# Three transformer blocks on one Trainium2 core: unread products ahead of TensorE's waits, sigmoid gates in one pass, compressed scores in two steps

## The reference, cut to what matters

```
# block 1: x = x + gate_m * (mixed @ w_out);  then x = x + gate_f * MLP(...)
fox = rms(forgetting_attention(q, k, v)) * gain * sigmoid(f_og)
ret = rms(retention(rope(rq), rope(rk), rv)) * gain * silu(r_gate)
# block 2 (NSA): x = layer_norm(ALPHA*x + mix); x = layer_norm(ALPHA*x + MLP(x))
s_c = q . kc ; p_c = masked_softmax(s_c) ; o = g0*(p_c @ vc) + g1*selected + g2*window
# block 3 (GLA): o = rms(gla(q, k, v)) * norm_g ; mix = (o * silu(r)) @ w_out ; norms as in block 2
```

## Time and profile before

| | |
|---|---|
| median of 3 runs | 1013.54 us (1010.81, 1013.54, 1016.82) |
| the profiled execution | 1010.89 us, span 1009.1 us |
| TensorE busy | 964.6 us, 96% of the span |
| VectorE busy | 655.6 us, 65% |
| ScalarE busy | 485.2 us, 48% |
| mean granted TensorE clock | 0.985 of full |
| DMA | 185 GB/s mean |

### The profile page before, as it was taken

The page is one execution under the profiler, slowest core; times in us unless marked ns, Lnnn a source line. Parts: engine busy times, 40 slices in busy tenths (PEclk is TensorE's granted clock), DMA queues, the critical chain, the costliest instruction groups (busy, mean ns, idle before and its releaser), DMA issues.

```text
span 1009.1 us, 14960 instructions
## 1 busy us (share of the span) xinstructions
PE 964.6 (96%) x5618; PEld 826.8 (82%) x5618; DVE 655.6 (65%) x830; ACT 485.2 (48%) x734; POOL 53.9 (5%) x59
## 2 busy tenths in 40 slices
PE   9999979799999999999799999998999989999996
PEld 7778867699999987876599999996776879999995
DVE  5977897784555656566865555557644876554555
ACT  5566736454544444444345444534544635444540
POOL 3040101100000001000100000001000010000000
PEclk9999989999999999999999999999999999999998
DMA  9989776596556666421385565554342547566531
GB/s 309 352 215 304 225 233 218 170 324 205 179 169 201 210 211 161 126 84 42 114 256 182 193 202 189 166 194 161 119 153 84 156 136 251 178 199 203 171 126 42
DMA packets 109991, 186.94 MB, mean 185 GB/s; under 512 B 8696, under 2 KB 67088, under 8 KB 109920
## 3 DMA queue, kind: packets, MB, share of 16 engines
q1 hardware_dynamic: 104800, 177.33, 54.5%
q0 software_dynamic: 2592, 8.53, 3.0%
q10 hardware_dynamic: 2544, 0.35, 0.2%
HBM read 185.13 MB, written 1.05 MB: 185 GB/s over the span
## 4 chain that ended last, share of the span: by engine, by line
PE 76%; DVE 10%; ACT 5%; issue 4%; DMA 3%; POOL 2%; SPq 0%; POOLq 0%; DVEq 0%; ACTq 0%
PE PJ L1774 14%; PE PJ L1775 13%; PE PJ L1776 13%; PE AT L1916 9%; PE AT L1915 9%; PE AT L1914 9%; DVE wlo L1110 2%; POOL rstd L470 2%; DMA raw<-in_w_in_dram 1%; PE AT L2000 1%; ACT whi L584 1%; PE AT L1765 1%; DMA raw<-in_w_out_dram 1%; ACT pr L807 1%; DVE bn L1198 1%
## 5 line engine op out<-in xcount | busy, mean ns | idle before, releaser
L1110 DVE TENSOR_TENSOR wlo<-raw,whi 128x1024 fp32r<-128x1024 f32 x144 | 172.8, 1221 | 51.8 <-ACT whi L584 51.3
L1914 PE MATMUL AT<-hT_hi,whi 128*128 128x256 f32 x720 | 203.8, 283 | 0.0
L1916 PE MATMUL AT<-hT_hi,wlo 128*128 128x256 f32 x720 | 203.7, 283 | 0.0
L1915 PE MATMUL AT<-hT_lo,whi 128*128 128x256 f32 x720 | 203.7, 283 | 0.0
L1241 DVE TENSOR_TENSOR wlo<-raw,whi 128x1024 fp32r<-128x1024 f32 x144 | 169.8, 1221 | 32.6 <-ACT whi L642 32.0
L1774 PE MATMUL PJ<-whi,uhi 128*128 128x512 f32 x432 | 171.1, 396 | 1.7 <-DVE wlo L1110 0.9
L584 ACT ACTIVATE whi<-raw 128x1024 fp32r<-128x1024 f32 x144 | 146.8, 1054 | 46.5 <-DMA raw<-in_w_in_dram 25.3
L1775 PE MATMUL PJ<-wlo,uhi 128*128 128x512 f32 x432 | 169.1, 391 | 0.0
L1776 PE MATMUL PJ<-whi,ulo 128*128 128x512 f32 x432 | 168.7, 391 | 0.0
L642 ACT ACTIVATE whi<-raw 128x1024 fp32r<-128x1024 f32 x144 | 144.4, 1049 | 47.2 <-PE PJ L1776 43.9
L1914 PEld LDWEIGHTS AT<-hT_hi,whi 128*128 128x128 f32 x720 | 138.0, 192 | 1.6
(11 more groups left out here) (315 smaller groups left out, 1080.4 us busy)
## 6 DMA issues: line engine op xcount, KB each, us to landing
raw<-in_mlp_w_dram SPq DMA_DIRECT2D x128, 512.0 KB, 4.8
raw<-in_w_in_dram SPq DMA_DIRECT2D x32, 512.0 KB, 6.4
raw<-in_w_ada_dram SPq DMA_DIRECT2D x32, 512.0 KB, 5.3
raw<-in_w_mlp_in_dram SPq DMA_DIRECT2D x32, 512.0 KB, 5.3
raw<-in_w_mlp_out_dram SPq DMA_DIRECT2D x32, 512.0 KB, 5.2
raw<-in_c_w_in_dram SPq DMA_DIRECT2D x24, 512.0 KB, 4.5
raw<-in_w_ada_dram SPq DMA_DIRECT2D x32, 256.0 KB, 6.4
raw<-in_a_w_in_dram SPq DMA_DIRECT2D x12, 512.0 KB, 5.0
```

The costliest lines, as they stand in the source:

```text
L1110: tt(wlo[:, n % SPL, :], raw_slot(r), whi[:, n % SPL, :].bitcast(F32), ALU.subtract).then_inc(raw_done, 1)
L1914: mm(o, whi[:, s % SPL, c], hT_hi[:, k, :], start=first, stop=False, skip_group_check=True)
L1915: mm(o, whi[:, s % SPL, c], hT_lo[:, k, :], start=False, stop=False, skip_group_check=True)
L1916: ins = mm(o, wlo[:, s % SPL, c], hT_hi[:, k, :], start=False, stop=last, skip_group_check=True)
```

## The change

- `busy(b, n)` issues n products of 128x256 in plain float32, identity by a constant, into AT bank b; nobody reads them. They have no wait of their own and stand ahead of waits: 5 ahead of `turn(2)`; 1, 2 and 4 at the start of the MLPs of blocks 2 and 3 (not of block 1); 2, 1 and 1 in the first column block of block 3 (`stage == 6`). These are 23 products.
- Gates: one ACT pass with the sigmoid function. The output gate's logits become column block 2 (`W_IN` swaps 1024 and 1536), so that the sigmoid takes the place of the copy out of PSUM; V becomes column block 3. DVE's `gate_min`, the second passes on ACT and the waits between them are gone. `gate_table` runs a one-column sigmoid ahead of the wait so that its table is loaded early.
- `cmp_scores` is called for tile 0 of the tokens behind weight tile 10 and for tile 1 behind weight tile 11; DVE's `cmp_max` and `cmp_probs` and ACT's `cmp_exp` move one step later.

```
-W_IN = [0, 512, 1024, 1536, 2056, 2568, 3080, 3592]
+W_IN = [0, 512, 1536, 1024, 2056, 2568, 3080, 3592]
...
+            def gate(z, e):
+
+                return nc.scalar.activation(e, z, ACT.Sigmoid)
+
+            def gate_table():
+
+                gate(cst[:, C_ID:C_ID + 1], junk[:, :])
...
             def fox_gates():
-                act.wait_ge(bank_free[1], 4)
-                gate_ln([proj[:, t, OG:OG + 512] for t in range(NT)], [proj[:, t, RV:RV + 512] for t in range(NT)])
+                act.wait_ge(w_used, T_IN + 12)
+                for t in range(NT):
+                    gate(bank(2, t), proj[:, t, OG:OG + 512]).then_inc(bank_free[0], 1)
+
+            def ret_gates():
+
+                gate_table()
+                act.wait_ge(w_used, T_IN + 32)
+                for t in range(NT):
+                    gate(bank(7, t), proj[:, t, RG:RG + 512]).then_inc(gt_sig, 1)
...
-                11: [lambda: block_out(2, T_IN + 12, FV)],
+                11: [fox_gates],
...
-                16: [lambda: probs_out(0), lambda: exps(2), lambda: block_out(3, T_IN + 16, OG)],
+                16: [lambda: block_out(3, T_IN + 16, FV), lambda: probs_out(0), lambda: exps(2)],
...
-                22: [lambda: fox_out(1), out_gates],
+                22: [lambda: fox_out(1)],
...
                 for t in range(NT):
                     o = proj[:, t, FK:FK + 512]
-                    gate_min(2 + t, bank(7, t), proj[:, t, RG:RG + 512])
+                    dve.wait_ge(gt_sig, t + 1)
                     tt(o, o, bank(7, t), ALU.mult).then_inc(bank_free[1], 1)
...
-                10: [lambda: maxima(6), cmp_max],
-                11: [gates_out, lambda: weigh(6), lambda: maxima(7), cmp_probs],
-                12: [lambda: maxima(8), lambda: probs_out(6), lambda: weigh(7)],
+                10: [lambda: maxima(6)],
+                11: [gates_out, lambda: weigh(6), lambda: maxima(7), cmp_max],
+                12: [lambda: maxima(8), lambda: probs_out(6), cmp_probs, lambda: weigh(7)],
...
+            def busy(b, n):
+
+                for _ in range(n):
+                    mm(AT[:, b, 0:S], ident, cst[:, C_TRI:C_TRI + S], start=True, stop=True)
...
                 for t in range(NT):
                     if t == 1:
+                        busy(3, 1) if stage == 6 else None
                         turn1()
+                    busy(*((1, 1) if t else (3, 2))) if stage == 6 else None
                     bank_wait(pb, t)
...
+                busy(3, 1) if m else None
                 transposes(stage, 1, src)
+                busy(3, 2) if m else None
                 up_first(0, 0)
+                busy(3, 4) if m else None
                 transposes(stage, 2, src)
...
+                busy(0, 5) if f == 2 else None
                 pe.wait_ge(rope_done, f + 1)
...
-                10: [lambda: S_(6), cmp_scores],
-                11: [lambda: S_(7)],
+                10: [lambda: S_(6), lambda: cmp_scores((0,))],
+                11: [lambda: S_(7), lambda: cmp_scores((1,))],
```

More of the change, by code:

```diff
@@ L210, in block_program @@
         bfor = sb("bfor", [P, 8])
+        junk = sb("junk", [P, 1])
         lf = sb("lf", [P, 6, 16])
@@ L255, in block_program @@
         dseq, aseq = sem("dseq"), sem("aseq")
-        gt_abs, gt_ln, gt_min, gt_sig = [sem(n) for n in ("gt_abs", "gt_ln", "gt_min", "gt_sig")]
+        gt_sig = sem("gt_sig")
         ffT_mm, ffT_done, ff_mm, ff_abs, ff_ln, ff_done, cum_mm, cum_done = [sem(n) for n in (
@@ L862, in _ @@
                 30: [lambda: mod_row_out(3)],
[L863 to L864 removed]
+                31: [ret_gates],
             })
@@ L981, in _ @@
                 10: [lambda: exps(6)],
-                11: [lambda: block_out(B_AIN + 2, T_AIN + 12, 1024, 280), branch_gates, lambda: exps(7), cmp_exp],
-                12: [lambda: exps(8)],
+                11: [lambda: block_out(B_AIN + 2, T_AIN + 12, 1024, 280), branch_gates, lambda: exps(7)],
+                12: [cmp_exp, lambda: exps(8)],
                 13: [lambda: nt_out(7, kT[0:64, 1536:2048]), cmp_out, lambda: exps(9)],
@@ L1049, in _, with r_gates @@
             r_at = lambda j, t: proj[:, t, 2048 + 512 * j:2048 + 512 * (j + 1)]
-            def r_ln(j):
+            def r_gates(j):
+                gate_table() if j == 0 else None
                 act.wait_ge(w_used, T_CIN + 20 + 4 * j)
-                gate_ln([bank(B_CIN + 4 + j, t) for t in range(NT)], [r_at(j, t) for t in range(NT)])
-            def r_sig(j):
                 for t in range(NT):
-                    gate_sig(4 + 2 * j + t, r_at(j, t))
+                    gate(bank(B_CIN + 4 + j, t), r_at(j, t)).then_inc(gt_sig, 1)
             tiles(T_CIN, T_COUT, {
@@ L1064, in _ @@
                 12: [lambda: g_out(3)], 15: [lambda: block_out(B_CIN + 3, T_CIN + 16, 1536)],
-                19: [lambda: r_ln(0), lambda: gla_squares(0)],
-                20: [lambda: r_sig(0), lambda: gla_squares(1)],
+                19: [lambda: r_gates(0), lambda: gla_squares(0)],
+                20: [lambda: gla_squares(1)],
                 22: [lambda: quarter_hi(7, 0), lambda: quarter_hi(7, 1)],
-                23: [lambda: hi_to(T_CIN + 27), lambda: r_ln(1), lambda: r_sig(1)],
+                23: [lambda: hi_to(T_CIN + 27), lambda: r_gates(1)],
             })
@@ L1379, in fox_final @@
                 link(tt(o, o, fgain, ALU.mult))
[L1380 to L1385, removed]
+                dve.wait_ge(bank_free[0], 4)
+                tt(o, o, proj[:, t, OG:OG + 512], ALU.mult).then_inc(src_ready, 1)
             def rotate(b, dst, k):
@@ L1556, in cmp_max @@
             def cmp_max():
-                dve.wait_ge(cs_mm, 1)
+                dve.wait_ge(cs_mm, 2)
                 link(tt(cs, AT[:, 0, 256:496].rearrange("p (t h c) -> p t h c", t=NT, h=8), m01, ALU.mult))
@@ L1695, in r_gain @@
                 for t in range(NT):
-                    dve.wait_ge(gt_abs, 4 + 2 * j + t + 1)
-                    ins = tt(out_at(j, t).rearrange("p (h d) -> p h d", h=2),
+                    dve.wait_ge(gt_sig, 2 + 2 * j + t + 1)
+                    tt(out_at(j, t).rearrange("p (h d) -> p h d", h=2),
                              logit(j, t).rearrange("p (h d) -> p h d", h=2),
[L1699 to L1704, removed]
-                    gate_min(k, logit(j, t), r_at(j, t))
-                    dve.wait_ge(gt_min, k + 1)
-                    dve.nop().then_inc(bank_free[j], 1)
+                             acc[:, NG:NG + 256].unsqueeze(1).broadcast_to([P, 2, 256]), ALU.mult).then_inc(bank_free[j], 1)
+                dve.wait_ge(bank_free[j], B_CIN + 4 + NT)
             def gla_norm(j, t):
@@ L1719, in gated @@
             def gated(j, t):
-                dve.wait_ge(gt_sig, 4 + 2 * j + t + 1)
+                dve.wait_ge(gt_sig, 2 + 2 * j + t + 1)
                 tt(out_at(j, t), out_at(j, t), r_at(j, t), ALU.mult).then_inc(src_ready, 1)
@@ L2095, in fox_values @@
                 if n == 0:
-                    pe.wait_ge(bank_free[0], 4)
+                    pe.wait_ge(bank_free[1], 4)
                 if n == 2:
@@ L2265, in compress2, with cmp_scores @@
                     .then_inc(c2_mm, 1)
-            def cmp_scores():
+            def cmp_scores(tiles):
                 pe.wait_ge(c2_done, 2)
                 pe.wait_ge(nt_done, 7)
-                for t in range(NT):
+                for t in tiles:
                     for h in range(8):
```

16 lines of the change are left out of this document (4 added, 12 removed).

## The result

The changed kernel takes 1003.13 us, the median of four runs (1002.46 to 1003.69), and the kernel before 1015.16 beside it. The ratio is 0.9899, with a 95% interval of 0.9868 to 0.9931: about 1% faster, and the range of 998.0 to 1008.5 holds the time. Two more samples, taken later beside the experiments, gave 0.9927 (0.9904 to 0.9950) and 0.9904 (0.9878 to 0.9930). The mean of all 16 executions is 1003.8 us. The profiled execution took 1002.46 us.

What follows compares the result with a forecast made beforehand. TensorE, busy 96% of the span and sometimes at half clock, was taken as the bound. From the profiled 1010.9 us, 3.2 + 1.8 + 2.0 + 2.9 - 0.6 + 0.3 = 9.6 gave 1001.3; plus 0.9, 1002 us, range 998 to 1008.5.

Steps and rivals of the forecast that it cites:

- compressed scores: Block 2's scores in two steps: no half-clock fall 1.6 us, group 7's exponentials 0.4; 2.0 us gained, bounds 0 and 2.4.
- Rival A: The clock falls anyway, everywhere; only earlier work counts: 2.5 us gained, 1008.4, or 1009.3 with the allowance; chance 0.12.
- C: Slower: fillers are exposed at 0.43 us each; 1008.3 without them, 1018.2 with all 23 exposed; chance 0.05.
- D: The gates give nothing because transfers hold the weight tiles: 1005.7 us; chance 0.13.
- B: Falls move to other places, block 1's norm or the border to block 3; two more at 1.5 us, 1005; chance 0.18.
- Rope and retention's gate: Rope: shorter first wait and clock kept by five products, 3.2 us; retention's gate: weight tiles earlier, 1.8 us.
- rival E: The fall stays at the rope alone, if two waits with only transposes between count as one pause: 1004; chance 0.10.
- MLP starts: Blocks 2 and 3: fillers in the waits keep the clock up, 1.4 and 1.5 us, together 2.9; bounds -0.2 and 3.2.
- First column block of block 3: Border to block 3: fillers stand behind the wait and cost 0.6 us; bounds 0.1 and -1.0.
- Block 3's gates: They end where TensorE does not wait; they free VectorE for the norm behind the output product: 0.3 us.
- Table loads: ScalarE: 9 instead of 13 at 1283 ns each; taken as no gain, since the new places lie in idle time.
- The allowance: 0.9 us added for clock falls at places left open, such as block 1's norm, since the profiled execution was lucky.

Runs made afterwards that it cites:

- experiment 9: Changed kernel without the 14 unread products at the MLP starts of blocks 2 and 3: 1006.12 us, ratio 0.9938 to the kernel before.
- experiment 7: Changed kernel with 46 unread products instead of 23: 1011.36 us, ratio 1.0001 to the kernel before.
- experiment 5: The changed kernel itself, unchanged, as a second sample: 1004.42 us, ratio 0.9927 to the kernel before; its profiled execution took 1007.89 us.
- Experiment 2: Kernel before the change with only the 23 unread products added: 1009.98 us, ratio 0.9974 to the kernel before.
- experiment 3: Changed kernel with the 16 products of compressed scores again in one go behind weight tile 10: 1006.61 us, ratio 0.9942.
- experiment 8: Changed kernel with four unread 128x128 transposes in place of each unread product: 1004.99 us, ratio 0.9936.
- experiment 4: Changed kernel without the four unread products in block 3's first column block: 1006.12 us, ratio 0.9939.
- experiment 1: Changed kernel without its 23 unread products, gates and compressed scores as changed: 1008.06 us, ratio 0.9958 to the kernel before.

## Why the prediction was right, and where it was off

The forecast held: 1003.1 us for 1002, in the main by the mechanism named. In the profiles it is 8.8 us for 9.6, and the terms did not all come out: the compressed scores brought 1.4 us less than forecast, block 3's mixer 0.8 more, and that these two partly cancel is luck. Rival A (the clock falls anyway) is out: without products it fell in 3 of 3 profiles at the border and at the MLP start of block 3, with unread work in none of 11. C (the products are exposed) is out: experiment 9 shows them free at block 2's MLP start, and experiment 7 what exposed ones cost. D (the gates give nothing) is out by the marks: 1.9 us between the rope and block 1's norm, as said below. (C and D put the gates at 3.5 us, while their terms add up to 3.3.) B came true only in part. One of the signs against the forecast did show, a fall behind filled waits, in 4 of 11 profiles at the rope; and the waits for weight tiles at the output product are 0.93 us in the profile (1.06 and 1.32 in the two later samples), not under 0.7.

*Price of a product*: ten passes take 2.32 us, as worked out. Added where waits are mostly full, 0.30 of the 0.43 us shows.

*Rope and retention's gate*, 3.2 and 1.8 us: up to block 1's norm the profile is 4.93 us earlier, for 5.0 predicted. Part of this closeness is chance: of the seven profiles with the new gates and no fall at the rope the first is the earliest at that norm, at 183.42 us; the others come at 183.78 to 185.13. Between the two marks the gain is 3.6. For the gate there is a comparison with the clock alike: the kernel before and experiment 5 both have 3.1 us of their half clock behind the first mark, and take 51.97 and 50.08 us. That is 1.9, for 1.8. (Experiment 2, with the old gates, takes 51.49 with 2.2 us of half clock behind its mark.) The clock is the rest, 1.7 us behind the mark, for 2.0 of which 0.4 lay ahead of it. Both waits came out as written (0.39 and 1.66). But the clock isn't safe there: it fell in 4 of 11 profiles with unread work. In three of these (experiments 3, 5 and 8) it had already fallen at 70 us; of the seven that held at the rope only experiment 4 had a fall there. Whether the two hang together was not tried. The half of rival E is true that the clock can still fall where the second wait is open. Its reason finds no support: the Trainium skill ("TensorE: Matmul & The Clock Gate", "Part 4: PE-mode transpose") says that transposes don't count as busy for the clock, and experiment 8, with nothing but transposes in the waits, had the same mean clock and the same three places kept at full speed. The measurement decides for this kernel. What in the second wait lets the clock fall in some executions wasn't tried by itself.

*Compressed scores*, 2.0 us: this is the step that failed, by its reason too. "I expect no fall" was wrong in 8 of 11 profiles with the scores in two steps, the first one among them. The term measured 0.6 us: 0 to 0.2 for the split as such (experiments 3 and 4). The other 0.4 is the wait for group 7's exponentials, which is gone in every later profile, with the scores in one go too (experiments 2 and 3), so it is not the split's. Nor is it shown that the split makes falls rarer: 3 of 3 profiles in one go and 8 of 11 in two steps are not told apart. The timeline of the changed kernel shows the two groups ahead of that fall:

```profile
411.00 1.85 PE L2256 MATMUL AT<-sc,qT 64*128 64x15 f32 x16
...
415.74 1.89 PE L2256 MATMUL AT<-sc,qT 64*128 64x15 f32 x16
```

I had read the stretch as the effect of one run of thin products without a pause. Halving the run doesn't prevent it, and four wider products among them don't either. What does decide there stays open: experiments 1, 7 and 8 had no fall, with the same code at this place. It is also the largest lever left, 1.6 to 4.8 us.

*MLP starts*, 2.9 us: 1.3 and 1.4 in the profile. (The products of 0.43 and 0.86 us exceed the wait of 1.02 by 0.27, not 0.15; it did no harm, 0.26 us of the next wait are left.) Products cost nothing there (experiment 9). Without them block 2's falls in only one of three profiles, so its gain is won in some executions only.

*First column block of block 3*, -0.6 us: sign and reason were wrong. The products there were to cost because they stand behind the wait and not in it; in truth they keep the clock up (0 of 11 against 3 of 3) and save 1.5 us over the fall as it comes in the new timing. Against the kernel before, whose fall at 685 us cost little, they give 0.1. I had priced the products and taken the clock as given.

*Block 3's gates*: 0.4 for 0.3. *Table loads*, taken as nothing: 9 instead of 13, as counted ahead; what they bring by themselves was not tried.

*The allowance* of 0.9 us for falls left open was called half of 2.65, which is 1.3; and 1.3 it is: the 16 executions have a mean 1.3 us above the profiled one. The places were those named in part: block 1's norm fell in 8 of 12 profiles where it was left unfilled, but costs 0.5 us at most there, since VectorE sets the end. As far as the profiles show, the allowance was spent at the rope, at the scores and perhaps at 70 us.

The gains add up to nearly the whole: the gates and scores alone 0.42%, the products alone 0.26%, together 0.68%, against 0.73 to 1.01% in the three samples. The rest is not told from chance by these intervals.

## What to carry to other kernels

Unread work of an engine in its wait for a slower one is free up to the length of the wait, and whether it pays is read from what comes behind: it pays where TensorE itself is the late one afterwards (MLP starts, the border to block 3), and gives nothing where the next wait takes the lost time back (block 1's norm). Beyond the waits the products cost: doubling them added 0.30 us for each of 0.43, and ate the whole gain. Don't judge such a change by one profile: split several at fixed marks of the program, and compare stretches of equal clock; in block 3's mixer and the MLPs of blocks 2 and 3 such stretches agreed within 0.1 us here, between the rope and block 1's norm within 0.4.

## What the runs showed of the hardware

- The same program has its stretches at half clock at different places in different executions: between 60 and 990 us one in the first profile of the changed kernel (at 417 us), five in the second.
- Unread transposes kept the granted clock as unread products did (0.989 on the mean of either, 1004.99 and 1004.42 us, experiments 8 and 5).
- In block 1's attention TensorE waits 0.4 us in one execution and 1.5 in another for the same copy on ScalarE. It goes back to ScalarE's wait ahead of it for a weight transfer at 80 us, which is 1.2 us longer as well: 3.9 us in the first sample of the changed kernel, 5.1 in experiment 1, in the rows of both for the stretch from 60 to 85 us:

```profile
ACT whi L585 <- DMA raw<-in_w_in_dram: 3.9, 1, 3.9
```

```profile
ACT whi L585 <- DMA raw<-in_w_in_dram: 5.1, 1, 5.1
```

This too makes single profiles differ by over 1 us before the rope.
